# Choosing and experts in one block, a shorter bit search, and the marking of slots spread over the experts

## What is computed

```
def expert_choice_moe(x, w_router, w_gate, w_up, w_down):
    num = b * n
    tokens = x.reshape(num, d)
    cap = CAPACITY_FACTOR * num // N_EXPERTS
    aff = jax.nn.softmax((tokens @ w_router).astype(jnp.float32), axis=-1)
    gates, idx = lax.top_k(aff.T, cap)
    xs = tokens[idx]
    hid = jax.nn.silu(jnp.einsum('ecd,edf->ecf', xs, w_gate)) * jnp.einsum('ecd,edf->ecf', xs, w_up)
    out = jnp.einsum('ecf,efd->ecd', hid, w_down) * gates[..., None].astype(x.dtype)
    y = jnp.zeros_like(tokens).at[idx.reshape(-1)].add(out.reshape(-1, d))
```

## Time and profile before

| | |
|---|---|
| time, median of 3 runs | 4718.57 us (4712.95 to 4734.83) |
| profiled execution, its own time | 4716.15 us |
| its span, first to last instruction | 4714.4 us |
| mean granted TensorE clock | 0.946 of full speed |
| PE busy | 4143.5 us (88%) |
| DVE busy | 2915.9 us (62%) |
| ACT busy | 2228.8 us (47%) |
| POOL busy | 1175.0 us (25%) |

### The profile page before, as it was taken

How to read it: one execution, slowest core, us unless ns; L and a number is a source line. 1 busy time by engine, 2 the same in 40 slices (tenths; PEclk the granted TensorE clock), 3 DMA queues, 4 the chain that set the end, 5 groups by cost and what they waited for, 6 DMA issues and landing times. The chain is left out here.

```text
span 4714.4 us, 123717 instructions
## 1 busy us (share of the span) xinstructions
PE 4143.5 (88%) x50861; PEld 3797.6 (81%) x50862; DVE 2915.9 (62%) x5152; ACT 2228.8 (47%) x4176; POOL 1175.0 (25%) x954
## 2 busy tenths in 40 slices
PE   6979999975999968888888869944999999999998
PEld 5869999965888856667676747734999999999998
DVE  5879999965888854444444447756444444444443
ACT  4568888854666633333333322201444444444443
POOL 4544444421344420110102223301112112112111
PEclk9989999998999979999999979966999999999999
DMA  8920000014444332222222246603556556556554
GB/s 167 187 61 26 22 23 26 23 32 136 144 153 143 127 133 67 66 66 64 67 64 67 60 124 203 196 25 95 168 175 180 170 172 184 168 171 184 170 172 108
DMA packets 555357, 540.74 MB, mean 115 GB/s; under 512 B 80320, under 2 KB 502464, under 8 KB 554944
## 3 DMA queue, kind: packets, MB, share of 16 engines
q1 hardware_dynamic: 489920, 435.44, 29.6%
q10 hardware_dynamic: 50240, 52.44, 4.9%
q0 software_dynamic: 14784, 46.57, 4.8%
HBM read 377.92 MB, written 156.43 MB: 113 GB/s over the span
## 5 line engine op out<-in xcount | busy, mean ns | idle before, releaser
L2298 DVE TENSOR_TENSOR g_wlo<-g_raw,g_whi 128x2048 fp32r<-128x2048 f32 x192 | 439.1, 2287 | 115.3 <-ACT g_whi L2260 115.3
L2260 ACT ACTIVATE g_whi<-g_raw 128x2048 fp32r<-128x2048 f32 x192 | 366.4, 1908 | 145.0 <-DMA g_raw<-expert_w_gate 145.0
L2369 PE MATMUL g_pD<-g_whi,g_hh 128*128 128x256 f32 x1536 | 417.3, 285 | 2.5 <-ACT g_o L2287 2.4
L2369 PE MATMUL g_pD<-g_wlo,g_hh 128*128 128x256 f32 x1536 | 408.1, 279 | 0.0
L1119 PE MATMUL c_pP<-c_xh,c_whi 128*128 128x258 f32 x1120 | 328.6, 293 | 34.7 <-DMA c_gup<-g_lora_up 29.3
L587 DVE TENSOR_TENSOR sapl<-sapT,saph 128x512 fp32r<-128x512 f32 x512 | 329.9, 686 | 2.7 <-ACT saph L546 2.7
L577 DVE TENSOR_REDUCE sanm<-sapS 128x1 f32<-128x1024 f32 x256 | 313.5, 1225 | 25.8 <-PE sapS L628 15.8
L2231 POOL DMA_INDIRECT g_x<-hn_rows,index x48 | 69.4, 1446 | 1035.2 <-PE g_pU L2353 1024.9
L546 ACT ACTIVATE saph<-sapT 128x512 fp32r<-128x512 f32 x512 | 278.8, 596 | 94.1 <-PE sapT L640 94.0
L1344 POOL TENSOR_TENSOR d_kr<-d_kr,d_fixed 128x512 f32<-128x512 f32 x80 | 101.8, 1273 | 880.0 <-ACT d_kr L1370 880.0
L1119 PE MATMUL c_pP<-c_xh,c_wlo 128*128 128x258 f32 x1120 | 319.9, 286 | 0.0
(11 more groups left out here) (369 smaller groups left out, 12445.8 us busy)
## 6 DMA issues: line engine op xcount, KB each, us to landing
g_raw<-expert_w_gate SPq DMA_DIRECT2D x64, 1024.0 KB, 5.0
g_raw<-expert_w_up SPq DMA_DIRECT2D x64, 1024.0 KB, 8.3
g_raw<-expert_w_down SPq DMA_DIRECT2D x64, 1024.0 KB, 5.0
ops<-c_ops SPq DMA_DIRECT2D x40, 1024.0 KB, 4.2
d_bd<-ops SPq DMA_DIRECT2D x160, 256.0 KB, 3.1
c_xh<-xT_hi SPq DMA_DIRECT2D x10, 1032.0 KB, 5.8
c_xl<-xT_lo SPq DMA_DIRECT2D x10, 1032.0 KB, 9.2
x_in<-x SPq DMA_DIRECT2D x20, 512.0 KB, 8.2
```

Source lines behind the costliest of these rows:

```text
L2260: act.activation(w_hi[:, Q % NBUF, :, :], raw[:, Q % NRAW, :, :], ACT.Copy).then_inc(s["g_hi"], 1)
L2298: dve.tensor_tensor(w_lo[:, Q % NBUF, :, :], raw[:, Q % NRAW, :, :], w_hi[:, Q % NBUF, :, :].bitcast(F32), ALU.subtract).then_inc(s["g_lo" ...
L2369: mm = pe.matmul(pD[k][:, 0:WB], x[:, d, k * P:(k + 1) * P], w[:, b, d, :], start=(d == 0 and i == 0), stop=(d == DC - 1 and i == len(part ...
```

## The change

`choose` and `experts` become one function with one block, `choose_and_experts`. Six things follow or go with it.

1. The barrier between them is gone. SP loads the first three weight blocks at the start of the merged block, before the affinities are written out; ACT rounds two blocks (`high(0)`, `high(1)`) right after the exponential, and DVE makes `low(0)` and `low(1)` before the first transposes.
2. In a search round, `cand` is made directly from the mask: `ahead`, which is the floor (the former `low`) with the next bit set, is prepared beforehand, and one instruction forms mask AND bit, OR `ahead`. The floor's own update and `ahead` are issued after the two comparisons, while PE counts.
3. `marked` and `found` are done before the first transposes for experts 0 and 1 only. Expert e + 2 is marked in the gate and up slices `j` = 0 to 6 of expert e, three tiles at a time; PE's 36 matmuls (`find`) for it stand at the start of down step `c` = 1, and `found` at the end of step 2.
4. `index` is made for each expert by itself, and `gather(e)` waits for its semaphore `f_ix`.
5. `hot` and `pI` are single instead of double; `pC` and `pP` share PSUM with `pD`, and `A` and `cum` share SBUF with `o[2]`.
6. The memset of the padding rows stands ahead of DVE's other set-up instructions.

```diff
@@ sync
             for Q in range(NE * NBK):
                 m, c = plan[Q % NBK]
+                if Q == NRAW:
+                    sp.wait_ge(s["f_sub"], 2)
+                    sp.dma_start(aff_rows.rearrange("(t p) e -> p t e", p=P), aff[:]).then_inc(s["f_st"], 16)
@@ gpsimd
+                else:
+                    pool.wait_ge(s["f_st"], 16)
+                pool.wait_ge(s["f_ix"], e + 1)
...
+            pool.wait_ge(s["g_pad"], 1)
             gather(0)
@@ scalar
+            act.wait_ge(s["f_sub"], 1)
+            act.activation(aff[:], aff[:], ACT.Exp).then_inc(s["f_exp"], 1)
             high(0)
+            high(1)
             for r in range(NTR):
                 turned(0, r)
-            high(1)
@@ vector, the search
             for r in range(BITS):
...
-                dve.wait_ge(s["f_count"], r + 1)
-                did(dve.tensor_scalar(mask[:], pC[:, 0:G2], float(CAP_S), -1.0, ALU.is_ge, ALU.mult))
-                did(dve.scalar_tensor_tensor(out=low[:], in0=mask[:], scalar=bit[:, r:r + 1], in1=low[:], op0=ALU.bitwise_and, op1=ALU.bitwise_or))
-                if r + 1 < BITS:
-                    did(dve.tensor_scalar(cand[:], low[:], bit[:, r + 1:r + 2], None, ALU.bitwise_or))
+                if r:
+                    did(dve.scalar_tensor_tensor(out=floor[:], in0=mask[:], scalar=bit[:, r - 1:r], in1=floor[:], op0=ALU.bitwise_and, op1=ALU.bitwise_or))
+                if r + 1 < BITS:
+                    did(dve.tensor_scalar(ahead[:], floor[:], bit[:, r + 1:r + 2], None, ALU.bitwise_or))
+                dve.wait_ge(s["f_count"], r + 1)
+                did(dve.tensor_scalar(mask[:], pC[:, 0:G2], float(CAP_S), -1.0, ALU.is_ge, ALU.mult))
+                into, other = (cand, ahead) if r + 1 < BITS else (floor, floor)
+                did(dve.scalar_tensor_tensor(out=into[:], in0=mask[:], scalar=bit[:, r:r + 1], in1=other[:], op0=ALU.bitwise_and, op1=ALU.bitwise_or))
@@ vector, marks and index
+            def marked(e, tiles):
+                if e and 0 in tiles:
+                    dve.wait_ge(s["f_id"], e)
...
+            def found(e):
+                dve.wait_ge(s["f_id"], e + 1)
+                dve.tensor_copy(two[:, e, :, :], pI[:, 0:6].rearrange("p (k n) -> p k n", n=2)).then_inc(s["f_idv"], 1)
+                dve.wait_ge(s["f_idv"], e + 1)
+                did(dve.scalar_tensor_tensor(out=idf[:, e, :], in0=two[:, e, :, 0], scalar=float(P), in1=two[:, e, :, 1], op0=ALU.mult, op1=ALU.add))
+                dve.tensor_copy(index[:, e, :], idf[:, e, :]).then_inc(s["f_ix"], 1)
@@ vector, ahead of the experts' loop
+            marked(0, range(NT))
+            found(0)
             low(0)
+            low(1)
+            marked(1, range(NT))
+            found(1)
             weights(0)
             for r in range(NTR):
                 turned(0, r)
-            low(1)
@@ vector, in the loop over j
                     low(NBK * e + j + 2)
+                    if e + 2 < NE and 3 * j < NT:
+                        marked(e + 2, range(3 * j, min(3 * j + 3, NT)))
@@ vector, in the loop over c
+                    if c == 2 and e + 2 < NE:
+                        found(e + 2)
@@ tensor
+            for e in range(2):
+                find(e)
             for r in range(NTR):
                 turn(0, r)
...
                 for c in range(NWB):
                     Q = NBK * e + FT_E + c
+                    if c == 1 and e + 2 < NE:
+                        find(e + 2)
                     pe.wait_ge(s["g_lo"], Q + 1)
```

More of the change, by code:

```diff
@@ L1975, with choose_and_experts @@
 FAR = 4096.0
-def choose(nc, logits, aff_rows, index):
+WB = 256
+NWB = F // WB
+SLOT = [(0, P), (1, P), (2, CAP_P)]
+def choose_and_experts(nc, logits, aff_rows, index, w_gate, w_up, w_down, hn_rows, out):
     with ExitStack() as ctx:
@@ L1985, in choose @@
         den = sb("f_den", [P, NT])
-        A = sb("f_A", [P, G2, TS])
         cnt = sb("f_cnt", [P, G2])
@@ L1990, in choose @@
         cap = sb("f_cap", [P, G2])
-        low = sb("f_low", [P, G2], I32)
+        floor = sb("f_low", [P, G2], I32)
         cand = sb("f_cand", [P, G2], I32)
+        ahead = sb("f_ahead", [P, G2], I32)
         bit = sb("f_bit", [P, BITS], I32)
@@ L2166 @@
-WB = 256
-NWB = F // WB
-SLOT = [(0, P), (1, P), (2, CAP_P)]
-def experts(nc, w_gate, w_up, w_down, hn_rows, aff_rows, index, out):
-    with ExitStack() as ctx:
-        sb, ps, sems = opened(nc, ctx)
         NBUF, NRAW, FT_E, NTR = 4, 3, F // P, 6
@@ new lines, in _ @@
+            dve.memset(notfirst[:].rearrange("p (g t) -> p g t", t=TS)[:, :, 0:1], 0.0)
+            did(dve.memset(A[:, NE:, TP:], -1.0))
+            dve.tensor_copy(onesb[:], onesf[:])
+            dve.wait_ge(s["f_c"], 5)
+            dve.tensor_copy(before[:], beforef[:])
+            dve.tensor_copy(slots[:], iota_i[:])
+            for k in range(2):
+                dve.tensor_copy(slots_p[:, k, :], iota_i[:, 0:CAP_P])
+            dve.tensor_copy(ids[:], ids_i[:])
+            did(dve.tensor_reduce(mxv[:], logits[:], AX.X, ALU.max))
```

226 lines of the change are left out of this document (93 added, 133 removed).

## The result

Measured side by side, the changed kernel took 4680.34 us (4669.14 to 4688.65, 4 runs) and the kernel before 4726.7 us (4712.95 to 4746.18, 4 runs): a ratio of 0.9917 [0.9888, 0.9945]. It is faster by 0.8%: its interval leaves out 1, but the change is small beside the 33 us over which the runs of before spread. The forecast of 4665 us is a ratio of 0.9887 to the 4718.57 known then, a hair outside that interval; the measured time lies, with 3 us to spare, inside the range of 4647 to 4683. All runs of this study together have a median of 4719.0 us before (54 runs, standard deviation 13.5) and 4666.4 us after (16 runs, 14.2).

What follows compares the result with a forecast made beforehand. PE was taken to bound the experts, DVE the marking, and a DVE-PE ring the search. Terms -7.8 - 56.2 + 0.9 + 10.8 = -52.3 us against 4716.15 gave 4663.9, stated as 4665 us; range 4647 to 4683.

Steps and rivals of the forecast that it cites:

- the way from the first index to the transposes: Between expert 0's index and PE's first transposes: transposes start at 3204.0 instead of 3260.15, -56.2 us.
- POOL's indirect DMA stands still until a run of such DVE instructions ends: First gather: two splits and expert 1's marks, 8.3 us in one DVE run, hold POOL until 3193.4.
- The search: Search rounds: one instruction leaves the DVE-PE ring, 0.27 us in each of 29 rounds, -7.8 us.
- they fit with 0.1 us to spare: Search round: floor update and `ahead`, 0.56 us together, fit in DVE's 0.67 us idle wait for the counts.
- The rival by which the search doesn't get shorter: Search: floor and `ahead` with their two waits reach past the counts, delaying the mask; 4673 us, chance 0.1.
- the first rival: First gather: DVE's run doesn't hold POOL (4657 us), or splits hold it and marks don't (4661 us); chance 0.2.
- the landing: Wait for the gates' data after the last gather issue: 3.4 us taken, between 3.4 and 6.2.
- The start of the block: The padding memset, now first on DVE ahead of the softmax: +0.9 us, between 0 and 0.9.
- The experts: Experts' loop: 36 matmuls on PE for each of 14 experts cost 0.77 us each, +10.8 us, bounds 2 and 20.
- The rival by which the pace follows the clock: Experts' loop: the 36 matmuls run faster at full clock, 0.28 instead of 0.77 us each; 4658 us, chance 0.15.
- The rival of PE's clock: Experts' loop: the sparse 36 matmuls lower PE's clock; 4691 or 5043 us; chance 0.03 cold spell alone, 0.02 slower kernel.
- The cover for the marks on DVE: Experts' loop: DVE's 2.6 us wait per slice for PE's up product hides the marks; cost 0, without it 62 us.

Runs made afterwards that it cites:

- `one_wait`: Changed kernel without DVE's own wait behind the instruction that makes `ahead` in the search rounds; 4666.0 us, ratio 0.9879.
- `rows_first`: `one_wait` with a separate semaphore for the gates' gathers, so PE's transposes wait for the rows' gathers alone; 4650.41 us, ratio 0.9855.
- `find_at_2`: Changed kernel with PE's 36 matmuls for expert e + 2 at the start of down step 2 instead of step 1; one execution, 4693.23 us.
- `find_twice`: Changed kernel with the 36 matmuls done twice in a row in the experts' loop; one execution, 4650.35 us.
- `marks_twice`: Changed kernel with a second, unread mark instruction for each tile marked in the experts' loop; one execution, 4656.7 us.
- `best`: Changed kernel with the edits of `one_wait` and `lows_late` together; 4651.68 us, ratio 0.9863.
- `rows_first_warm`: `rows_first` with 54 extra, unread matmuls of 256 columns in PE's two waits ahead of the first transposes; 4649.68 us, ratio 0.9847.
- `lows_late`: Changed kernel with DVE's two weight splits put behind expert 1's marks and index and an increment after POOL's first gather; one execution, 4668.03 us.

## Why the prediction was right or wrong

**The forecast for the change itself held to 3 us, but two steps of the prediction failed: one term inside the sum, and the step from the sum to a time.** The touched part gave -55.2 us in the means of two and three traces, summed were -52.3. The term is the way from the first index to the transposes, by "POOL's indirect DMA stands still until a run of such DVE instructions ends": the last gather was to be issued 17.3 us after PE's first 36 matmuls, and was after 12.0. That the total is still near comes in part of luck, since the misses have both signs. Cast on the whole time the forecast was a ratio of 0.9887; the later two measurements gave 0.9869 and 0.988, and all runs together 4666.4 against 4719.0.

**From the sum to a time: the larger miss, 15 us from 4665 to 4680.34.** I took the one profiled execution of before as the frame ("the median of the runs stands 2.4 us above the profiled one") and let the range come from the bounds of the terms alone. The 22 us over which the runs of before spread were named for what a measurement can tell, and not put into the range. The traces show the largest part of it: the clock of a stage 2000 us ahead of the change, at 0.85 in one execution and 0.58 in another, and 24 us from it. Another 20 to 23 us of scatter at either level lie ahead of the change too; where, was not looked into. The profile of before was an execution at the short level. That of the changed kernel was at the long one, and the four runs of the first measurement had mean clocks of 0.941, 0.942, 0.943 and 0.946 at 4688.7, 4682.6, 4678.1 and 4669.1 us, while nine of the twelve later ones had 0.949 to 0.953 at 4647 to 4667. By the clock at least three of those four were at the long level. The difference of the first measurement, 46 us, is therefore not the size of the change, and I don't explain it by anything in the change: code ahead of it is the same, and both levels occur among the runs of the changed kernel. Why a given execution gets the one or the other stays open; six of the seven traces at the long level and five of the seven at the short one are of kernels with the merged block, which shows no link.

**The search: -5.6 instead of -7.8.** Which instruction leaves the ring was right, and so was that the floor and `ahead` fit behind the comparisons. The step that was mis-sized is "they fit with 0.1 us to spare": the instructions alone leave 0.22 us, and what was put at nothing is the second wait that now stands in front of the mask. `one_wait` has it at 0.07 us a round, 2.1 us in all, and without it the round is the 1.74 us that were forecast. The rival by which the search doesn't get shorter names these two waits, but its mechanism, that they reach past the counts, is not what happened: DVE stayed idle for 0.29 us, and the cost was a quarter of the rival's.

**From the first index to the transposes: -60.4 instead of -56.2.** Three steps are in it. That POOL is held was right. That it is held until the run of DVE instructions ends, marks included ("I take that they do, because the only rows of such a meeting are of it") was wrong in both halves: one split holds one indirect DMA and lets it in before the next, 2.24 and 1.74 us, and the marks don't hold it at all, 0.91 us. The first gather was 2.2 us long instead of 8 to 9, and the last issue ended 3211.98 + 0.94 - 3200.90 = 12.0 us after the start of PE's first 36 matmuls, where the forecast had 3200.6 - 3183.29 = 17.3. These 5.3 us belong to the first rival, in its half where the splits hold and the marks don't (it had put 3.8 us on it), whose chance of 0.2 was too low: the nearest row was of another kind of instruction. The Trainium skill (SBUF — State Buffer, Who interferes with whom), weighed in the prediction, is half borne out: `tensor_tensor` with both inputs in SBUF holds POOL (2.24 against 0.91 us), and that `tensor_scalar` can hold it too doesn't show in the marks' form. The third step, the landing, was 4.4 us instead of 3.4 (between my bounds of 3.4 and 6.2). The 3.4 us were those of a direct store on a quiet queue. The gates' gather landed with the DMA engines full of rows and of two weight blocks. `rows_first` shows that the rows were only 1.3 us ahead of the gates, so that it is not the gates alone that had to be priced. How much of the landing the two weight blocks cost, which the prediction let pass as "at most two blocks", stays open.

**The start of the block: +0.5 instead of +0.9,** within its bounds of 0 and 0.9; not looked into further.

**The experts: +9.0 in the first pair, +10.0 between the means of three traces each (1432.9 without the marks, 1442.9 with them), predicted +10.8.** The price of the 36 matmuls was the measured pace of 27 ns; at clock 1.00 it is 25.3 to 25.5. By the timeline each one costs 1.04 us from the matmul ahead to the one behind, where the gap had been 0.41: +0.63 instead of +0.77, 14 times 8.8 us. `find_at_2` confirms that the gap is used, `find_twice` the price. The rest of the +10.0, 1.2 us, is not of the loop. It lies in the first slice, whose cold gate group all three traces of the changed kernel have and only one of the three others (5.44, 5.63 and 5.85 us against 5.41, 3.79 and 3.79). From the second slice's gate group to the last scatter it is 1433.8 to 1434.1 us against 1425.0 to 1425.2, +8.8. The rival by which the pace follows the clock would have given 14 x 0.28 = +4, and falls. The rival of PE's clock falls too, at 1.00 throughout. The cover for the marks on DVE was there, as `marks_twice` shows with twice their number.

Against the first pair's -56.3 the misses add up so: POOL brought 5.3 us more than summed, the loop 1.8, the start 0.4; the landing took back 1.0 and the search 2.2. That is 4.3 us more, and 4.0 were found.

**A little is left.** `one_wait`, `best`, `rows_first` and `rows_first_warm` have touched parts of 1554.0 to 1556.1 us against 1557.8 to 1559.8, in the means 3.9 us less. 2.1 of it are the wait, 0.4 the one long round. Their whole times (ratios 0.9847 to 0.9879) can't be told from those of the changed kernel.

## What to carry to other kernels

Compare two traces first at the point where the changed code begins, and put the scatter of what lies ahead of it into the range of the forecast: here the part that the change touches repeated within 2 us, and the part in front of it within 51. A serial stretch on one engine at the end of a stage can go into the slack of the next, and what it then costs is only what it puts on the engine that sets the time there; the standing gaps of that engine are the places for it. Before a landing is priced, look for the transfers that the change starts beside it. In a ring of two engines count the waits in front of the instruction that closes it, not only its instructions.

## What the hardware showed that was not expected

- A second wait in front of an instruction, satisfied before the first, made it start 0.07 us later (DVE, 0.29 against 0.22 us idle, 1.807 against 1.733 us a round, nearly all rounds alike).
- Between two `tensor_tensor` splits that follow each other at once on DVE (4.48 us for two), POOL's indirect DMA gets in; it doesn't wait for the end of the run. In the earlier trace rows it took 3.13 us, as if it had waited; what differs there was not tried.
- The marks, `tensor_scalar` from and to bf16, didn't hold POOL (0.91 to 1.21 us), but sixteen of them took 3.56 us beside its gathers in `lows_late`, and 3.24 and 3.22 where fewer or none ran.
- Matmuls of two bf16 columns followed each other at 25.3 ns with the clock at 1.00 and at about 27 at 0.50: nearly the same, whatever the clock.
- An increment that POOL makes behind six indirect DMAs in its own order came in the second of them, and DVE passed its wait while two were still to be made (`lows_late`); as a sign that they are issued it can't be used.
- In the changed kernel's wait for the gathered data the DMA engines were full (DMA share 1.06 over 7 us), of 1.3 MB of rows and two weight blocks of 1 MB, and the gates' last packet came 1.2 us behind the rows'.
- The granted clock of one and the same stage was 0.80 to 0.85 in some executions and 0.58 in others, and cost 24 us. The first gate group began at or near clock 0.50 in ten traces and at 1.00 in four, which was worth 1.7 us. Extra matmuls raised it in a wait of PE (0.78), and it was gone again 8 us later, at the end of sparse transposes (PE busy for 4.8 of 8 us).
